# Mixer 1 attention with low keys on 128 rows, values as the stationary operand in two column groups, and one flat run of 48 steps per layer

## The chip, the cores and the metric

The kernel runs on one core of one Trainium2 chip, as one program. The metric is the device time of that core in microseconds (us), taken as the median of several executions. The names of the engines are those of the profile: PE is TensorE, PEld its weight loads, DVE is VectorE, ACT is ScalarE, POOL is GpSimd, SP is the queue from which the weights are fetched.

## The reference, cut to what matters

A sequence of 512 tokens of width 1024 goes through two layers of a first block and one layer of a second block, all in float32. Each layer of the first block is feed-forward, mixer, feed-forward, each behind an RMS norm:

```
x = x + 0.5 * swiglu(rmsnorm(x), gate, up, down)
proj = rmsnorm(x) @ w_in       # 256 pool columns, then q, k, v of 12 heads of 64
q, k = rope(q), rope(k)        # first 16 of the 64 channels
y = [pool(v_pool), attention(q, k, v)]
x = x + y @ w_out
x = x + 0.5 * swiglu(rmsnorm(x), gate2, up2, down2)
```

The attention of a head is a mixture of three dilated windows. The kernel computes it as one softmax over all 512 keys: exp(scale * (q.k + band)), where band holds the logarithm of how many of the three windows see a key, divided by the sum of those exponentials, times v. The second block (a gated part and a sparse attention) has its own code and isn't touched but for its norms.

## The kernel before, in words

Activations stand transposed, with channels on the 128 partitions and the 512 tokens along the free side, in 8 tiles (`x`, `xh`, `xl`). Every weight matrix is cut into units of 128 output columns by 1024 input rows. A unit is fetched by SP, split by POOL into a high part `wh` (L445) and a low part `wl` (L448) in two slots that alternate, and multiplied on PE in 8 blocks of three matmuls (L462 to L464: high times high, high weights times low activations, low weights times high activations). POOL may overwrite a slot once the unit before in that slot is used (`unit_used`). A layer has 66 units of the first feed-forward, 20 of the mixer's input projection (units 0, 1, 2 are q, k, v of head pair 0, units 3 and 4 the pool channels, then q, k, v of pairs 1 to 5), 8 of the output projection and 66 of the second feed-forward. Order on every engine is the order of the program; engines meet through semaphores only.

**Norm.** Before each projection ACT squares the 8 tiles of `x` into `sq` (SBUF, 4 buffers, L901), DVE adds them up in `rstd` (L1188, L1192), PE sums over partitions with a matmul with ones (`sum_of_sums`, L475, placed after the first four blocks of unit 2), and DVE and ACT make the inverse root in `rstd` (L1180, L905, L1182). In the mixer DVE also sets `padded` and `win` to zero ahead of the norm (L1415, L1416).

**Start of the mixer.** DVE makes `cosr` and `sinr`, turns q and k of pair 0 (`rope`: one product with `cosr`, L1263, four of 32 rows with `sinr`, L1266, one sum, L1271), evacuates v (L1294) and the two pool tiles (L1303), and forms the low parts `low_q` (L1280) and `low_k` (L1288) from the high parts that ACT has made (L927, L934). PE first does units 0 to 4. `proj_read` tells PE which banks were read.

**A pair of heads** is `pair_steps`, 8 steps: steps 0 to 3 are the four query tiles of head 0, steps 4 to 7 those of head 1. In a step PE computes the scores of 128 queries against 512 keys by two matmuls (`scores`): L588 with `qs` against `ks`, all 128 rows, which hold high and low queries above high keys twice, and L590 with the 64 rows of high queries against the 64 rows of `kl`. DVE adds the band and takes the row maximum (L1348), and negates it (L1351). ACT exponentiates with a row sum (L955). PE transposes the result in four tiles (`turn`, L597), ACT copies it to `pt` (L948), and PE multiplies with `pt` as weights and the 64 columns of `vtok` moving (`values`, L609), which gives 64 columns of bank 7 with tokens on partitions. Between these PE does the three units of the next pair in 24 blocks (`fill`), in counts of 3, 3, 3, 2, 2, 2, 1, 1 and, behind step 7, 2, 2, 1, 2. Turns trail scores by two steps and values by three. At the end of a pair the pipeline runs empty: the last turns and values, DVE's reciprocal and scaling (L1375, L1378), and PE's `turn_back` to channels (L562), which ACT and DVE split into `mh1` and `ml1` (L978 or L982, L1389). Pairs 0 to 3 are two passes of a hardware loop with two pairs in it; pair 5 has no fill. Then comes the output projection (`out_blocks`).

## Time and profile before

| | us |
|---|---|
| median of 3 runs (2848.26 to 2851.93) | 2850.3 |
| span of the profiled execution | 2847.3 |
| PE busy | 2701.1 (95%) |
| DVE busy | 1351.3 (47%) |
| ACT busy | 548.1 (19%) |
| POOL busy | 1477.8 (52%) |

Only the span is given for the profiled execution; what lies around it is taken as the difference to the median, 3.0 us. The page's chain that ended last puts 84% of the span on PE, 9% on DVE, 2% on ACT and 1% on POOL. The first layer's mixer lies between about 385 and 705 us of the span, the second layer's between about 1428 and 1746 us. In a row of the timeline the first two numbers are the start and the time in us, and brackets at the end give the engine's idle time just before and what ended it. PE's rows overlap, because its matmuls are pipelined: the cost of one is the distance between its start and the next one's. A call on float32 data (not the split kind) appears as two matmuls.

### The profile page before, as it was taken

The page shows a single profiled execution, that of the slowest core. Times are in us where ns is not written, and L with a number is a line of the kernel's source. Part 1 is how long each engine was busy: PE and PEld are TensorE (multiplying, and loading weights), DVE is VectorE, ACT ScalarE, POOL GpSimd, SP SyncE. Part 2 cuts the span into 40 slices and gives each one's busy share as a digit, 9 for nine tenths or more (in the row PEclk, how much of TensorE's full clock was granted, in tenths as well). Part 3 has the DMA queues.
Part 4 walks back from the last instruction along what each step waited for, and adds up shares of the span by engine and source line. Part 5 has one row for each costly group of instructions (what it writes and reads, how often), then busy time and mean ns, then how long its engine had stood idle before and what let it go on. Part 6 is the DMA issues. An engine that isn't in the chain of part 4 may idle for free.

```text
span 2847.3 us, 35053 instructions
## 1 busy us (share of the span) xinstructions
PE 2701.1 (95%) x12380; PEld 2179.0 (77%) x12380; DVE 1351.3 (47%) x1812; ACT 548.1 (19%) x996; POOL 1477.8 (52%) x828
## 2 busy tenths in 40 slices
PE   6999989989999999999989999999989889999998
PEld 5888867767888878888867768888866667788886
DVE  5555055564555215553075655555044566555512
ACT  2110014432111002110033432110021255211100
POOL 4666652225666656666642226666643400566663
PEclk9999999999999999999999999999999989999999
DMA  3222220111222222222210102222232200222221
GB/s 140 97 95 103 88 89 30 44 45 60 95 97 100 92 104 74 103 89 103 93 70 30 44 30 91 101 95 97 103 117 84 73 3 0 74 98 94 103 88 74
DMA packets 34366, 228.48 MB, mean 80 GB/s; under 512 B 5364, under 2 KB 6132, under 8 KB 7412
## 3 DMA queue, kind: packets, MB, share of 16 engines
q1 hardware_dynamic: 33140, 226.23, 22.0%
q10 hardware_dynamic: 1152, 1.29, 0.1%
q8 instruction: 43, 0.70, 0.1%
q14 instruction: 31, 0.25, 0.0%
HBM read 225.41 MB, written 2.10 MB: 80 GB/s over the span
## 4 chain that ended last, share of the span: by engine, by line
PE 84%; DVE 9%; issue 4%; ACT 2%; POOL 1%; DMA 0%; DVEq 0%; SPq 0%; ACTq 0%; POOLq 0%
PE bank L462 24%; PE bank L463 24%; PE bank L464 24%; PE bank L609 2%; DVE ropet L1266 1%; PE bank L590 1%; POOL wl L448 1%; DVE rstd L1192 1%; PE bank L839 1%; DVE qs L1280 1%; PE bank L597 1%; PE bank L588 1%; ACT ks L934 1%; DVE rstd L1182 1%; PE bank L712 1%
## 5 line engine op out<-in xcount | busy, mean ns | idle before, releaser
L445 POOL TENSOR_SCALAR wh<-raw 128x1024 fp32r<-128x1024 f32 x412 | 443.2, 1076 | 1307.4 <-PE bank L464 1227.8
L448 POOL TENSOR_TENSOR wl<-raw,wh 128x1024 fp32r<-128x1024 f32 x412 | 1034.8, 2512 | 34.4
L462 PE MATMUL bank<-xh,wh 128*128 128x512 f32 x2096 | 844.1, 403 | 15.9 <-DVEq L1306 10.9
L463 PE MATMUL bank<-xl,wh 128*128 128x512 f32 x2096 | 825.3, 394 | 0.0
L464 PE MATMUL bank<-xh,wl 128*128 128x512 f32 x2096 | 824.8, 394 | 0.0
L462 PEld LDWEIGHTS bank<-xh,wh 128*128 128x128 f32 x2096 | 398.5, 190 | 118.4 <-issue 32.0
L464 PEld LDWEIGHTS bank<-xh,wl 128*128 128x128 f32 x2096 | 398.5, 190 | 84.4
L463 PEld LDWEIGHTS bank<-xl,wh 128*128 128x128 f32 x2096 | 399.1, 190 | 79.9 <-issue 2.6
L464 PE MATMUL bank<-acth,wl 128*128 (+1 forms) x880 | 342.9, 390 | 0.0
L463 PE MATMUL bank<-actl,wh 128*128 (+1 forms) x880 | 342.9, 390 | 0.0
L462 PE MATMUL bank<-acth,wh 128*128 (+1 forms) x880 | 342.9, 390 | 0.0
L1203 DVE SCALAR_TENSOR_TENSOR x<-bank,x 128x512 f32<-128x512 f32 x64 | 43.9, 691 | 607.6 <-PE bank L464 607.6
L1231 DVE TENSOR_TENSOR un<-gn,un 128x512 f32<-128x512 f32 x110 | 310.1, 2819 | 0.0
L1221 DVE TENSOR_TENSOR un<-bank,rstd 128x512 f32<-128x512 f32 x110 | 76.0, 691 | 472.0 <-PE bank L464 472.0
L920 ACT ACTIVATE gn<-gn 128x512 f32<-128x512 f32 x110 | 69.6, 632 | 961.3 <-DVE gn L1221 961.3
L464 PEld LDWEIGHTS bank<-acth,wl 128*128 128x128 f32 x880 | 165.3, 188 | 34.3
L462 PEld LDWEIGHTS bank<-acth,wh 128*128 128x128 f32 x880 | 165.3, 188 | 34.2
L463 PEld LDWEIGHTS bank<-actl,wh 128*128 128x128 f32 x880 | 165.3, 188 | 34.0
L609 PE MATMUL bank<-vtok,pt 128*128 128x64 f32 x768 | 101.0, 277 | 29.7 <-ACT pt L948 28.5
L1230 DVE TENSOR_TENSOR acth<-gn,un 128x512 f32 (+1 forms) x110 | 123.8, 1126 | 0.0
L609 PEld LDWEIGHTS bank<-vtok,pt 128*128 128x128 f32 x768 | 96.6, 198 | 34.6 <-ACT pt L948 32.8
L1348 DVE CUSTOM_DVE_ANT_0 sc<-bank,band 128x512 f32<-128x512 f32 x96 | 66.4, 691 | 107.3 <-PE bank L590 104.2
(211 smaller groups left out, 2483.0 us busy)
## 6 DMA issues: line engine op xcount, KB each, us to landing
raw<-in_stream SPq DMA_DIRECT2D x206, 1024.0 KB, 4.8
x<-in_x SPq DMA_DIRECT2D x2, 1024.0 KB, 9.5
w<-in_w1k SPq DMA_DIRECT2D x1, 2048.0 KB, 8.1
w<-in_w1v SPq DMA_DIRECT2D x1, 2048.0 KB, 7.7
out_dram<-x SPq DMA_DIRECT2D x4, 512.0 KB, 2.7
invcount<-in_c_invcount ACTq DMA_DIRECT2D x1, 512.0 KB, 14.7
wst<-in_ws SPq DMA_DIRECT2D x1, 512.0 KB
band<-in_c_band ACTq DMA_DIRECT2D x1, 448.0 KB, 13.6
```

The lines of the kernel that those rows point to most:

```text
L445: nc.gpsimd.tensor_scalar(wh[:, h, :, :], src, 1.0, 1.0, ALU.mult, ALU.mult)\
L448: nc.gpsimd.tensor_tensor(wl[:, h, :, :], src, wh[:, h, :, :].bitcast(F32), ALU.subtract).then_inc(split_done, 1)
L462: mm = nc.tensor.matmul(bank, wh[:, slot, k, :], rh, start=start, stop=False)
L463: mm = nc.tensor.matmul(bank, wh[:, slot, k, :], rl, start=False, stop=False)
L464: return nc.tensor.matmul(bank, wl[:, slot, k, :], rh, start=False, stop=stop)
L609: mm = nc.tensor.matmul(B[7][:, c:c + HD], pt[:, s % 2, kt * P:(kt + 1) * P], vtok[:, e, kt, HD * a:HD * (a + 1)], start=(kt == 0), stop=( ...
L920: nc.scalar.activation(gn[:, e, :], gn[:, e, :], ACT.Silu).then_inc(silu_done, 1)
L1203: V.scalar_tensor_tensor(x[:, m, :], B[m][:, :], factor, x[:, m, :], ALU.mult, ALU.add)\
L1221: V.tensor_tensor(dst[:, e, :], B[2 * e + j][:, :], rstd[:, :], ALU.mult)\
L1230: V.tensor_tensor(h, gn[:, e, :], un[:, e, :], ALU.mult).then_inc(act_part, 1)
L1231: V.tensor_tensor(un[:, e, :], gn[:, e, :], un[:, e, :], ALU.mult).then_inc(act_part, 1)
L1348: V.tensor_tensor_reduce(sc[:, s % 4, :], B[(5, 2)[s % 2]][:, :], band[:, off:off + T], 1.0, -3.0e38, ALU.add, ALU.max, smax[:, s:s + 1]). ...
```

## The change

- **Scores.** `kl` becomes `[P, 2, 2, T]`: for each head its low keys lie in that head's 64 rows and the other 64 rows are zero. The second matmul takes all 128 rows of `qs`. POOL sets `kl`, `padded` and `win` to zero in each layer, between its split of units 67 and 68; DVE's two memsets go.
- **Values.** The 64 columns of `vtok` of a head are now the weights, and two turned tiles (256 queries) of `pt` or `sq` move. A half of a pair (4 steps) is 8 calls, heads alternating, into partitions 0 to 63 and 64 to 127 of bank 7. Steps go query tile by query tile, heads alternating in them.
- **Normalising.** Since the output has channels on partitions at once, the reciprocals are spread (`recb`, ACT), transposed by PE (`reciprocal_rows`), and multiplied by DVE with a copy of bank 7 that ACT has made (`on`, `numerators`, `normalise`). Low outputs are formed from two SBUF tiles (`low_output`).
- **Order.** The 48 steps of a layer run through without a break and without loops. Values, reciprocals and outputs of a pair are done within the steps of the next one. Fill is 4, 4, 4, 4, 2, 2, 2, 2. The evacuation of v and of the pool tiles moves from ahead of the first scores to behind the first maxima. The ten pool operations are spread over pairs 1 to 4. `sc` has 3 buffers for 4.
- **Norm.** All norms but two (6 and 9) put the squares into three free PSUM banks; DVE copies the first and adds seven.

```diff
-        kl = sb("kl", [P, 2, T], F32R, at=mix1)
+        kl = sb("kl", [P, 2, 2, T], F32R, at=mix1)
@@ POOL
-            with pool.Fori(0, U_ALL // 4) as i:
+            def split_units(i):
...
+            with pool.Fori(0, DEPTH) as l:
+                with pool.Fori(0, U_FFN // 4 + 1) as i:
+                    split_units(l * (U_LAYER // 4) + i)
+                nc.gpsimd.memset(kl[:, :, :, :].bitcast(F32), 0.0).then_inc(zeroed, 1)
+                nc.gpsimd.memset(padded[:, :, :], 0.0).then_inc(zeroed, 1)
+                nc.gpsimd.memset(win[:, :, :], 0.0).then_inc(zeroed, 1)
+                with pool.Fori(U_FFN // 4 + 1, U_LAYER // 4) as i:
+                    split_units(l * (U_LAYER // 4) + i)
@@ PE
-                        nc.tensor.matmul(B[(5, 2)[s % 2]][:, :], qs[h:h + HD, e, a, i:i + P], kl[h:h + HD, e, :],
-                                         start=False, stop=True).then_inc(s_done, 1)
+                    nc.tensor.matmul(o[:, :], qs[:, e, a, i:i + P], kl[:, e, a, :], start=False, stop=True)\
+                        .then_inc(s_done, 1)
+                def values(h):
+                    j, half = h // 2, h % 2
+                    if half == 0:
+                        pe.wait_ge(vtok_done, l * PAIRS + (j + 1))
+                        pe.wait_ge(num_done, l * PAIRS + (j + 1))
+                    pe.wait_ge(pte_done, l * STEPS + (4 * h + 6))
+                    q = 2 * P * half
+                    for kt in range(NQ):
+                        for a in range(2):
+                            r = slice(HD * a, HD * (a + 1))
+                            mm = nc.tensor.matmul(B[7][r, q:q + 2 * P], vtok[:, j % 2, kt, r], turned(h)[:, 4 * a + kt, :],
+                                                  start=(kt == 0), stop=(kt == NQ - 1))
+                    mm.then_inc(pv_done, 1)
+                for j in range(PAIRS):
+                    work = [(n, k) for n in range(3) for k in range(KT)] if j < PAIRS - 1 else []
                     for s in range(8):
+                        g = 8 * j + s
+                        if s == 0 and work:
+                            fill(j, work, FILL[s])
+                        scores(g)
+                        if s > 0 and work:
+                            fill(j, work, FILL[s])
                         if s == 1:
+                            value_turn(j)
+                        if g >= 2:
+                            turn(g - 2)
+                        if s == 2 and j > 0:
+                            values(2 * j - 1)
+                        if s == 3 and j > 0:
+                            reciprocal_rows(j - 1)
+                        if s == 6:
+                            values(2 * j)
+                        if j == PAIRS - 1 and s in (4, 5):
+                            pooled_map(s - 4)
+                turn(STEPS - 2)
+                turn(STEPS - 1)
...
                 pe.wait_ge(ml_done, l * 8 + 8)
-                out_blocks(0, range(KT - 1))
-                turn_back(l * PAIRS + 5)
-                out_blocks(1, range(4))
+                out_blocks(0, range(4))
+                values(HALVES - 1)
+                out_blocks(0, range(4, KT - 1))
+                reciprocal_rows(PAIRS - 1)
+                out_blocks(1, range(KT - 1))
@@ DVE, norm: to is the tuple of free banks
-                V.tensor_tensor(rstd[:, :], sq[:, 0, :], sq[:, 1, :], ALU.add).then_inc(sq_used, 2)
-                for m in range(2, KT):
+                V.tensor_copy(rstd[:, :], B[to[0]][:, :]).then_inc(sq_used, 1)
+                for m in range(1, KT):
-                    V.tensor_tensor(rstd[:, :], rstd[:, :], sq[:, m % 4, :], ALU.add).then_inc(sq_used, 1)
+                    V.tensor_tensor(rstd[:, :], rstd[:, :], B[to[m % 3]][:, :], ALU.add).then_inc(sq_used, 1)
@@ DVE, behind the maximum of step s of pair j
+                        if s == 0:
+                            v_out(l * PAIRS + j, ...)
+                        if j == 0 and s < 2:
+                            pool_out(s)
+                        if s == 1 and j > 0:
+                            reciprocals(j - 1)
+                        if s == 4 and j > 0:
+                            normalise(j - 1)
+                        if s in (2, 3) and more:
+                            rope(pair, 0, u, B[slot], s - 2)
+                        if s in (4, 5) and more:
+                            rope(pair, 1, u + 1, B[1 - slot], s - 4)
+                        if s == 5 and more:
+                            low_q(pair, 1 - e)
+                        if s == 6 and j > 0:
+                            low_output(j - 1, j)
                         if s == 7 and more:
+                            low_k(pair, 1 - e)
+                        if s in (0, 1, 6) and 1 <= j <= 4:
+                            n = (j - 1) * 3 + (0, 1, 6).index(s)
+                            if n < len(pool_ops):
+                                pool_op(n)
@@ ACT, behind the exponential of step s of pair j
+                        if s == 1 and j > 0:
+                            spread_reciprocals(j - 1)
+                        if s == 3 and j > 0:
+                            numerators(j - 1)
+                        if s == 4 and more:
+                            high_q(l * PAIRS + (j + 1), 1 - e)
+                        if s == 5 and j > 0:
+                            high_output(j - 1)
+                        if s == 6 and more:
+                            high_k(l * PAIRS + (j + 1), 1 - e)
```

## Rows read from the trace of the kernel before

**Rows 1.** Windows: stretch and length, busy of PE, PEld, DVE, ACT, POOL, PEclk, DMA share, GB/s.
```profile
433.50:651.70 218.20, 203.35 (x1076) 156.36 (x1074) 128.69 (x257) 90.26 (x188) 53.52 (x30) 0.94 0.11 39
429.40:434.00 4.60, 4.51 (x10) 3.15 (x10) 2.74 (x4) 1.12 (x1) 0.00 (x0) 0.50 0.00 0
```
**Rows 2.** Timeline of PE, step 3 of pair 1, and the next scores.
```profile
484.47 0.48 PE L588 MATMUL bank<-ks,qs 128*128 128x512 f32 x1
484.88 0.50 PE L590 MATMUL bank<-kl,qs 64*128 64x512 f32 x1
485.31 0.50 PE L462 MATMUL bank<-xh,wh 128*128 128x512 f32 x1
485.65 0.40 PE L463 MATMUL bank<-xl,wh 128*128 128x512 f32 x1
485.89 0.39 PE L464 MATMUL bank<-xh,wl 128*128 128x512 f32 x1
...
486.81 0.60 PE L597 MATMUL bank<-ident,sc 128*128 128x128 f32 x4
487.24 1.00 PE L609 MATMUL bank<-vtok,pt 128*128 128x64 f32 x8
488.06 0.48 PE L588 MATMUL bank<-ks,qs 128*128 128x512 f32 x1
```
**Rows 3.** Timeline of PE, pair ends with their idle time, and two starts in pair 5.
```profile
506.59 1.97 PE L609 MATMUL bank<-vtok,pt 128*128 128x64 f32 x8 [2.79 <-ACT pt L948]
...
545.35 1.11 PE L609 MATMUL bank<-vtok,pt 128*128 128x64 f32 x8 [0.65 <-ACT pt L948]
...
641.83 0.48 PE L588 MATMUL bank<-ks,qs 128*128 128x512 f32 x1
643.96 0.48 PE L588 MATMUL bank<-ks,qs 128*128 128x512 f32 x1
```
**Rows 4.** The chain of waits, in order of time: start, us, what.
```profile
2187.09 7.05 PE bank L712 x32
```
**Rows 5.** Timeline of PE: two diagonal tiles, and two column groups in blocks of eight.
```profile
634.23 1.08 PE L634 MATMUL bank<-padded,poolw_now 64*64 64x512 f32 x4
2226.33 2.57 PE L761 MATMUL bank<-wst,gvtok 128*64 128x128 f32 x32
```
**Rows 6.** Groups by line, 433.5 to 632.5: count, busy us, mean ns, idle before.
```profile
L955 ACT ACTIVATE sc<-sc,sneg 128x512 f32<-128x512 f32 x40 | 28.7, 718 | 26.1 <-DVE sneg L1351 26.0
L1348 DVE CUSTOM_DVE_ANT_0 sc<-bank,band 128x512 f32<-128x512 f32 x41 | 28.3, 691 | 46.3 <-PE bank L590 44.9 <-DVE qs L1280 0.9
```
**Rows 7.** Timeline of DVE at the end of pair 1.
```profile
493.68 4.31 DVE L1280 TENSOR_TENSOR qs<-qk,qs 64x512 fp32r<-64x512 f32 x2
...
506.09 1.40 DVE L1288 TENSOR_TENSOR kl<-qk,ks 64x512 fp32r<-64x512 f32 x2 [2.65 <-ACT ks L934]
```
**Rows 8.** Line L1192 by itself: ns min/median/max, first and last start.
```profile
L1192 DVE TENSOR_TENSOR rstd<-rstd,sq x48: 691/693/2759, 28.0 to 2475.5; 128x512 f32<-128x512 f32 x48
```
**Rows 9.** Timeline at the start of mixer 1, first layer: DVE, then PE.
```profile
394.12 0.94 DVE L1415 MEMSET padded<- 128x1056 f32 x1 [0.17 <-issue]
...
405.96 1.25 PE L475 MATMUL bank<-rstd,ones 128*128 128x512 f32 x2 [3.94 <-DVE rstd L1192]
429.49 0.79 PE L462 MATMUL bank<-xh,wh 128*128 128x512 f32 x1 [7.17 <-DVEq L1306]
```
**Rows 10.** Timeline of ACT ahead of the first scores.
```profile
426.63 2.58 ACT L934 ACTIVATE ks<-qk 64x512 fp32r<-64x512 f32 x4 [4.16 <-DVE qk L1271]
```
**Rows 11.** POOL: the split of unit 68 (timeline), and the page's group of low parts.
```profile
394.77 1.05 POOL L445 TENSOR_SCALAR wh<-raw 128x1024 fp32r<-128x1024 f32 x1 [5.34 <-PE bank L487]
...
L448 POOL TENSOR_TENSOR wl<-raw,wh 128x1024 fp32r<-128x1024 f32 x412 | 1034.8, 2512 | 34.4
```
**Rows 12.** Timeline of PE at the start of block 2.
```profile
2133.14 1.24 PE L475 MATMUL bank<-rstd,ones 128*128 128x512 f32 x2 [2.65 <-DVE rstd L1192]
2149.54 9.53 PE L712 MATMUL bank<-w,blk 128*62 128x256 f32 x32 [5.51 <-DVE blk L1532]
```

More of the change, by code:

```diff
@@ L556, in mixer1, with fill @@
                     unit_blocks(u0 + n, n % 2, bank, range(KT))
-                def turn_back(pair):
-                    pe.wait_ge(otok_done, pair + 2)
+                def fill(j, work, count):
+                    slot = (1 + j) % 2
+                    for n, k in [work.pop(0) for _ in range(count)]:
+                        if k == 0:
+                            pe.wait_ge(proj_read, l * U_PROJ + (2 if j == 0 and n < 2 else j * 3 + (4 + n)))
+                        unit_blocks(u0 + (5 + j * 3 + n), (slot + n) % 2, B[(slot + n) % 2], [k])
@@ L965, in pair_steps @@
+                        if s == 4 and more:
[4 more added lines that the diff above has]
+                            high_k(l * PAIRS + (j + 1), 1 - e)
+                        if s >= 6 and not more:
+                            t = s - 6
                             act.wait_ge(poolmm_done, l * 2 + (t + 1))
@@ L1341, in pair_steps, with low_output @@
+                def low_output(j, done):
+                    dve.wait_ge(mh_done, l * 8 + done)
+                    V.tensor_tensor(ml1[:, 2 + j, :], on[:, :], mh1[:, 2 + j, :].bitcast(F32), ALU.subtract)\
+                        .then_inc(ml_done, 1)
+                for j in range(PAIRS):
+                    e, more = j % 2, j < PAIRS - 1
+                    pair, u = l * PAIRS + (j + 1), u0 + (5 + j * 3)
+                    slot = (1 + j) % 2
                     for s in range(8):
-                        i = s % 4
@@ L1355, in pair_steps @@
-                        if s == 6 and more:
-                            low_q(pair + 1, 1 - e)
-                        if s == 7 and more:
-                            rope(pair + 1, 1, u + 1, B[1 - slot], 0)
-                        for n in range(len(pool_ops) * s // 8, len(pool_ops) * (s + 1) // 8) if pooled else ():
-                            after, o, in0, in1, op = pool_ops[n]
-                            dve.wait_ge(pool_step, ps + after)
-                            V.tensor_tensor(o, in0, in1, op).then_inc(pool_step, 1)
@@ L1363, in pair_steps @@
-                        if s in (4, 6) and not more:
-                            t = s // 2 - 2
-                            dve.wait_ge(mh_done, l * 8 + (t + 6))
-                            V.scalar_tensor_tensor(ml1[:, t, :], B[t][:, :], poolscale_now[:, t:t + 1],
-                                                   mh1[:, t, :].bitcast(F32), ALU.mult, ALU.subtract)\
-                                .then_inc(ml_done, 1)
-                    if more:
-                        rope(pair + 1, 1, u + 1, B[1 - slot], 1)
-                        low_k(pair + 1, 1 - e)
@@ L1381, in pair_steps @@
-                    if more:
-                        v_out(pair + 1, u + 2, B[slot])
-                def output(done, at):
-                    h, lo = mh1[:, at, :], ml1[:, at, :]
-                    if not isinstance(at, int):
-                        h, lo = h.rearrange("p a t -> p (a t)"), lo.rearrange("p a t -> p (a t)")
-                    dve.wait_ge(mh_done, done)
-                    V.tensor_tensor(lo, B[6][:, :], h.bitcast(F32), ALU.subtract).then_inc(ml_done, 1)
-                with dve.Fori(0, 2) as it:
-                    for e in range(2):
-                        pair_steps(it * 2 + e, e, True)
-                        output(l * 8 + it * 2 + (e + 1), bass.ds(it * 2 + (2 + e), 1))
@@ new lines, in mixer1 @@
+                        if s == 7 and more:
+                            low_k(pair, 1 - e)
[3 more added lines that the diff above has]
+                                pool_op(n)
+                        if s == 7 and not more:
+                            pool_low(0)
+                pool_low(1)
+                reciprocals(PAIRS - 1)
+                normalise(PAIRS - 1)
```

337 lines of the change are left out of this document (152 added, 185 removed).

## The prediction

> **What bounds the kernel now.** The page comes first: PE is busy 95% of the span and holds 84% of the chain that ended last, so time goes only where PE's own work shrinks or where PE stands idle. The windows come second. In the first layer's attention, 433.5 to 651.7, PE is busy 203.4 of 218.2 us, at a mean granted clock of 0.94 of full speed [rows 1]. So 14.8 us are idle, and some of the rest runs at the lower of the two levels, 1.2 GHz instead of 2.4: the stretch behind the first wait stands at 0.50 over 4.6 us [rows 1], so each such stretch loses about 2.3 us. Third is the timeline of one step, read by the distances of starts [rows 2]. In plain blocks a matmul costs 0.23 to 0.24 us (485.65 to 485.89; 0.23 below). The first scores matmul costs 0.41, the second, on 64 rows, 0.43, and the block's first one behind it 0.34. The four transposes cost 0.43 (486.81 to 487.24), the values of one step 0.82 (487.24 to 488.06). Fourth are the waits at the ends of pairs: 2.79 and 0.65 us idle [rows 3]. Behind 2.79 the eight value matmuls show 1.97 us and behind 0.65 only 1.11, so the long wait also cost the clock and the short one did not.
>
> As a check, the ledger of these 48 steps before: scores and the block behind 48 x 1.18, of which 0.23 belongs to the block, 45.6; 117 blocks x 0.69, 80.7; turns 48 x 0.43, 20.6; values 48 x 0.82, 39.4; turns of v and of outputs 11 x 0.36 (an estimate, a little under the 0.43 of the same four transposes), 4.0; two pool maps 2.5, from 1.08 each [rows 5] and a start. That makes 192.8. With 14.8 idle and four to five clock losses of 2.3 it gives 217 to 219, against 218.2.
>
> **Scores.** Both matmuls now fill 128 rows, as do the blocks around them. I price them as blocks: 0.46 a step instead of 0.95, so 48 x 0.46 = 22.1 instead of 45.6, 23.5 less a layer. The bounds are 0.46 and 0.95 (if what costs is something other than the 64 rows); I take the first, because everything else in the sequence that is 128 by 128 and split runs at 0.23 [rows 2].
> The Trainium skill, TensorEngine Tiling (Array Packing), Key Properties, says that a change of the tiling mode drains TensorE. By that rule the extra 0.49 us is two drains a step and goes, as I have it; but the rule also puts two drains around each half of the values.
>
> **Values.** A half is 8 calls, 16 matmuls of 256 moving columns. The same width on 62 weight columns takes 7.05 us for 32 [rows 4], 0.220 each, with weight loads hidden: 3.53 a half one after the other, 1.76 if the two column groups run fully side by side. Two rows bear on that [rows 5]. The pool map has two 64x64 tiles on the diagonal, four matmuls of 512 columns, which at the same rate would be 1.76 in series; it shows 1.08. Two column groups of 128x64 in blocks of eight show 2.57 for 32 matmuls of 128 columns, where the rate makes 3.53. So they do overlap, and the more they alternate the more so; here they alternate with every call. I take 1.76 and 0.39 for entry and exit (0.18 and 0.11 above the plain 0.23 in rows 2, and 0.1 for the lone first matmul), 2.15 a half. Eleven of the twelve halves lie in the 48 steps (23.7), the last between the output blocks. Twelve make 25.8 for 39.4: 13.6 less a layer. Ends: 1.76 and 3.92.
> The Trainium skill, TensorE: Matmul & The Clock Gate, The mechanism, states that a weight load overlaps running matmuls only where the row group differs, and here both heads use all rows; by that each matmul would pay its load too. The row of 62 weight columns contradicts it, since 0.220 a matmul leaves no room for a load between them, and I give it no chance.
>
> **The rest of PE's work.** Pair 0's first four blocks now come ahead of scores 0, so 116 blocks remain, 80.0. Turns stay 20.6, small turns 4.0, pool maps 2.5. Sum of the 48 steps: 22.1 + 80.0 + 20.6 + 23.7 + 4.0 + 2.5 = 152.9.
>
> **What waits then.** ACT needs about 1.5 a step, 0.72 for the exponential [rows 6] and by estimate 0.2 for reading its sum and 0.6 for a copy of the same width; that is 12 of 28 us a pair and 6 more for its other copies: no bound. DVE needs about 0.95 a step for maximum and negation [rows 6], and 0.69 for every operation that reads a bank: 7.6 + 12 x 0.7 for both ropes + 1.4 + 1.4 for the low parts + 0.7 each for v, normalising and low output + 2.5 to 3.5 of pool operations, 24 us a pair. With two SBUF operands it takes 0.69 alone and 2.76 beside POOL's low part [rows 8]; `low_q` took 4.31 for two [rows 7]. So 24 to 28 us against PE's 28.6: near, and it matters how it lies. The late half is tight. Put scores 4 of a pair at 0. PE's steps 4, 5 and 7 have two blocks (0.46 + 1.38 + 0.43 = 2.27), step 6 has 4.42 with values, and four blocks (2.76) stand ahead of the next scores: these could start at 14.0. DVE does maximum 4 to 1.6, normalises to 2.3, three rope reads to 4.4, maximum 5 to 5.4, two rope reads and the sum to 7.6, `low_q` to 9.1, maximum 6 to 10.0. ACT exponentiates to 11.0 and makes the high keys, 2.58 [rows 10], to 13.6. `low_k` takes 1.4 [rows 7]: 15.1. That is 1.1 us late. POOL splits the next unit from about 11 to 14.5, so `low_k` or the pool operation ahead may run slow; I take 2.0 us a boundary, between 0 and 4.9. An idle of 2.0 is nearer 0.65 without clock loss than to 2.79 with it [rows 3], less clearly than I would like. Five boundaries: 10. In the last pair, without fill, a step took 2.13 (641.83 to 643.96 [rows 3]); shorter scores leave ACT's 1.5 and the round trip, 1.65 by estimate. Its eight steps and pool parts come to 17 for 14.5 of work, 2.5 idle, and 1.2 more until the second pool tile's low part lets the output blocks start. Sum: 152.9 + 10 + 3.7 = 166.6, and 2.15 for the last half behind: 168.8 against 218.2, 49.4 less. The second layer repeats the first within 1 us. Two layers: 98.8.
>
> **Ahead of the attention.** PE waits 3.94 us for DVE's sum of squares [rows 9]. Its adds take up to 2.76 beside POOL [rows 8], behind two memsets that begin at 394.1 [rows 9]. A read of a bank takes 0.69 [rows 6], some 0.78 with its semaphore. Eight from 394.1 end at 400.3, before PE gets there at 402.0 (405.96 - 3.94). The wait goes, no more: 3.9, and about 0.4 because the sum's own matmuls (1.25 for two) no longer run at the lower clock, an estimate. Then v and the pool tiles leave the path: high keys end at 426.63 + 2.58 = 429.2 [rows 10], `low_k` at 430.7, and scores started at 433.5, so 2.8 less. PE still idles before its first fill (7.17 us before [rows 9]): v's evacuation no longer counts there but q's and k's banks do, so it idles about 4.5, and four slow blocks end just before `low_k` does. Start: 7.1 a layer, 14.2 in all.
> POOL's three memsets, 4160 elements a partition, stand in its idle 5.34 us [rows 11]. At POOL's fastest row, 1.05 us for 1024, they take 4.3 and fit; at its slower one, 2.51 for 1024 [rows 11], 10.2, which holds unit 68 back by 4.9 and eats the 3.9. A plain write is nearer the first, so 0.
> Block 2's norm saves PE's 2.65, and DVE's chain to the next wait of 5.51 moves with it [rows 12]: 2.7. The feed-forward norms gain nothing: PE has blocks to do there and shows no wait at its sum. Longer straight code on all engines: nothing, since no long wait of the trace names instruction fetch.
>
> **Sum.** 98.8 + 14.2 + 2.7 = 115.7. The profiled execution spans 2847.3; with the 3.0 between span and median, 2850.3 - 115.7 = 2734.6, say 2735.
>
> **Rivals.**
> 1. *The column groups don't overlap.* A half costs 3.92. For it: two groups in blocks of eight saved only 27% of the series. Against it: the diagonal tiles. 24 x 1.77 = 42 more: 2777.
> 2. *DVE is late at every boundary and the clock goes with it.* Idle 4.9 instead of 2.0, and 2.3 of lower level, ten times: 52 more, 2787. For it: DVE's 24 to 28 of 28.6 us, `low_q` at 4.31. Against: POOL has its split done before `low_q`.
> 3. *The scores gain nothing*, what costs is not the 64 rows: 47 more, 2782. Against it: the jump from 0.23 to 0.41 is seen nowhere between tiles of one shape in rows 2.
> 4. *Slower.* Short waits in every step hold the granted clock at the lower level through the attention. PE's 152.9 become 305.8; with the same waits and last half that is 324 a layer against 218.2, 106 more, twice 212, less 17 for starts and norm: 3045. It needs 0.50 as in rows 1 over the whole stretch; it decides from about 37% of the work (168.8 + 0.37 x 152.9 exceeds 218.2 + 7.1). Against it: the last pair waits a little in every step and its scores still show 0.48, the full speed's value [rows 3].
>
> **How the numbers follow.** Forecast 0.66 with its own range of 2708 to 2765 (boundaries 0 to 20 less, or 15 more; memsets up to 9 more; last pair 6 either way); rival 1 0.11, rival 2 0.13, rival 3 0.07, rival 4 0.03. The range of 2700 to 2785 takes in 1 and 3 and part of 2. A measurement tells 0.2%, about 6 us, from no change; only rival 4 lies beyond, and only a mild form of it near zero: faster 0.96, same 0.01, slower 0.03.
>
> **What would show it.** The attention stretch of about 169 us with the last half, at a clock near 0.97. Scores' two starts 0.23 apart; 16 value matmuls within 2.2 us (3.9 would be rival 1). L475 in both mixers without a wait and eight DVE reads of 0.69 before it. POOL idle between memsets and unit 68. PE idle at scores of step 0 behind `kl`, 1 to 3 us; over 4 with half-speed blocks behind it would be rival 2. A time above 2785 or below 2700 would mean that a term of this sum is wrong by a third.

## The result, and the profile after

The changed kernel takes 2745.5 us (median of 4 runs, 2743.2 to 2751.3) against 2849.6 for the kernel before on the same chip, a ratio of 0.9639 [0.9627, 0.9651]. The forecast was 2735, with an own range of 2708 to 2765. The forecast started from 2850.3, the median of three runs before; the profiled execution of the changed kernel took 2747.0, 103.3 less than that. The spans of the two profiled executions differ by 102.1, where 115.7 was forecast.

First the page of the changed kernel: the span, the busy times, and the chain that ended last by engine.

```profile
span 2745.2 us, 34077 instructions
...
PE 2612.7 (95%) x11996; PEld 2109.0 (77%) x11996; DVE 1314.9 (48%) x1816; ACT 559.2 (20%) x1018; POOL 1480.5 (54%) x834
...
PE 84%; DVE 7%; issue 4%; ACT 2%; POOL 2%; DMA 0%; DVEq 0%; SPq 0%; ACTq 0%; POOLq 0%
```

PE still bounds the kernel: it is busy 95% of the span and holds 84% of the chain, both as before. Where the 102.1 came from is read by setting the same events of both traces side by side, PE's starts in us (the last column is the difference of the two lengths):

| stretch | before | after | change | forecast |
|---|---|---|---|---|
| up to mixer 1, layer 1 | 389.48 | 388.64 | -0.8 | 0 |
| start of mixer to first scores, layer 1 | 44.0 | 34.8 | -9.2 | -7.1 |
| the same, layer 2 | 41.8 | 34.8 | -7.0 | -7.1 |
| first scores to output blocks, layer 1 | 218.3 | 174.3 | -44.0 | -51.6 |
| the same, layer 2 | 218.6 | 174.3 | -44.3 | -51.6 |
| output blocks to feed-forward 2, layer 1 | 49.8 | 53.8 | +4.0 | +2.15 |
| the same, layer 2 | 49.8 | 56.5 | +6.7 | +2.15 |
| the four later feed-forward stretches together | | | -1.3 | 0 |
| block 2 to its first L734 (L712 before) | 36.2 | 32.3 | -4.0 | -2.7 |
| rest of block 2 | | | -2.2 | 0 |

So the direction of every large term is right. The attention gained 7.3 to 7.6 us a layer less than forecast, and the stretch behind it cost more than forecast.

Windows of the changed kernel: stretch and length, busy of PE, PEld, DVE, ACT, POOL, PEclk, DMA share, GB/s. The first answers to [rows 1].

```profile
423.40:597.70 174.30, 159.30 (x865) 122.07 (x865) 122.67 (x260) 93.70 (x198) 54.52 (x30) 0.97 0.14 49
...
482.00:486.00 4.00, 3.71 (x13) 3.00 (x14) 2.68 (x7) 1.41 (x3) 0.00 (x0) 0.68 0.00 0
574.00:582.00 8.00, 4.87 (x17) 3.85 (x18) 4.41 (x10) 3.50 (x8) 1.69 (x1) 0.60 0.36 131
```

PE is busy 159.3 of 174.3 us, at 0.97 of the full clock against 0.94. The idle time is still 15.0, as before (14.8): the waits moved and did not go. Two short stretches stand at the lower level in part, 482 to 486 and 574 to 582. Before there were four in this layer's attention (from 468, 506, 584 and 622) and the end of one that began ahead of it.

The timeline of PE in the changed kernel: start, us, instruction, idle time just before. It answers to [rows 2].

```profile
459.87 1.95 PE L631 MATMUL bank<-sq,vtok 128*64 128x256 f32 x16
461.75 0.50 PE L600 MATMUL bank<-ks,qs 128*128 128x512 f32 x1
...
560.98 0.48 PE L600 MATMUL bank<-ks,qs 128*128 128x512 f32 x1
561.29 0.39 PE L601 MATMUL bank<-kl,qs 128*128 128x512 f32 x1
561.52 0.40 PE L489 MATMUL bank<-xh,wh 128*128 128x512 f32 x1
...
562.91 0.60 PE L616 MATMUL bank<-ident,sc 128*128 128x128 f32 x4
563.26 0.48 PE L600 MATMUL bank<-ks,qs 128*128 128x512 f32 x1
```

A step with two blocks takes 563.26 - 560.98 = 2.28 us; the forecast had 2.27. Inside it the first scores matmul costs 0.31, the second 0.23 and the block's first one 0.23, together 0.77; before the three cost 0.41, 0.43 and 0.34, together 1.18. Whether the 64 rows are the cause of that is tested below. A half of the values costs 461.75 - 459.87 = 1.88, and 2.09 with the longer turn ahead of it (0.53 for 0.35) and the 0.02 that the scores behind it are dearer; the forecast had 2.15.

The same timeline, now the rows with idle time. It answers to [rows 3].

```profile
451.03 0.49 PE L600 MATMUL bank<-ks,qs 128*128 128x512 f32 x1 [1.92 <-DVE kl L1326]
...
482.29 0.49 PE L600 MATMUL bank<-ks,qs 128*128 128x512 f32 x1 [2.21 <-DVE kl L1326]
...
484.00 0.63 PE L489 MATMUL bank<-xh,wh 128*128 128x512 f32 x1
...
546.20 0.49 PE L600 MATMUL bank<-ks,qs 128*128 128x512 f32 x1 [2.16 <-DVE kl L1326]
...
577.08 0.79 PE L600 MATMUL bank<-ks,qs 128*128 128x512 f32 x1 [4.63 <-DVE kl L1326]
...
596.24 0.66 PE L616 MATMUL bank<-ident,sc 128*128 128x128 f32 x4 [1.14 <-ACT sc L994]
597.67 0.49 PE L489 MATMUL bank<-mh,wh 128*128 128x512 f32 x1 [0.78 <-DVE ml L1380]
...
614.45 0.50 PE L489 MATMUL bank<-mh,wh 128*128 128x512 f32 x1 [3.05 <-POOL wl L463]
```

At four boundaries PE waits 1.9 to 2.2 us for the low keys (at 515.01, not shown, 2.10); the forecast had 2.0. At the fifth it waits 4.63 and then works at half speed. Behind the wait of 2.21 it does too (the row of a block's matmul shows 0.63 at 484.00, and 0.39 to 0.40 at full speed), behind those of 1.92, 2.10 and 2.16 it does not. In the second layer the four waits are 1.95, 2.17, 2.05 and 2.19, and there it is the one of 2.05, at 1506.29, that has half-speed blocks behind it. Last, it waits 3.05 for POOL in the output blocks, where 1.11 stood before.

What is late there is read from the timelines of DVE, ACT and POOL at the fifth boundary.

```profile
562.22 0.69 DVE L1408 CUSTOM_DVE_ANT_0 sc<-bank,band 128x512 f32<-128x512 f32 x1 [1.21 <-PE bank L601]
...
569.10 1.40 DVE L1318 TENSOR_TENSOR qs<-qk,qs 64x512 fp32r<-64x512 f32 x2
570.72 0.69 DVE L1408 CUSTOM_DVE_ANT_0 sc<-bank,band 128x512 f32<-128x512 f32 x1 [0.22 <-PE bank L601]
...
574.96 1.99 DVE L1326 TENSOR_TENSOR kl<-qk,ks 64x512 fp32r<-64x512 f32 x2 [1.92 <-ACT ks L959]
...
571.64 0.72 ACT L994 ACTIVATE sc<-sc,sneg 128x512 f32<-128x512 f32 x1 [2.91 <-DVE sneg L1411]
...
572.36 2.57 ACT L959 ACTIVATE ks<-qk 64x512 fp32r<-64x512 f32 x4
...
573.35 2.35 POOL L463 TENSOR_TENSOR wl<-raw,wh 128x1024 fp32r<-128x1024 f32 x1
```

The chain is the one of the forecast: maximum 4, the ropes, `low_q`, maximum 6, exponential 6, high keys, low keys. `high_k` needs only `qk`, which was ready at 569.0, but it stands behind exponential 6 in ACT's order, and ACT is idle 2.91 us ahead of that. `low_k` ends at 576.95, 14.7 us behind maximum 4's start and 16.0 behind the scores of step 4 (560.98); its first part runs beside POOL's `wl` (1.99 for 1.40).

### The profile page after: what moved, and what is told of

It is laid out like the page before. It is cut to its first block, busy times and chain, and to the rows that moved or that the text cites. A ratio compares the mean times of both kernels' runs of the same rounds, so it can differ in the third digit from the quotient of the medians.

```text
span 2745.2 us, 34077 instructions
## 1 busy us (share of the span) xinstructions
PE 2612.7 (95%) x11996; PEld 2109.0 (77%) x11996; DVE 1314.9 (48%) x1816; ACT 559.2 (20%) x1018; POOL 1480.5 (54%) x834
## 4 chain that ended last, share of the span: by engine, by line
PE 84%; DVE 7%; issue 4%; ACT 2%; POOL 2%; DMA 0%; DVEq 0%; SPq 0%; ACTq 0%; POOLq 0%
PE bank L489 25%; PE bank L491 25%; PE bank L490 25%; POOL wl L463 1%; PE bank L631 1%; DVE ropet L1304 1%; PE bank L861 1%; PE bank L616 1%; PE bank L600 1%; ACT ks L959 1%; PE bank L601 1%; DVE rstd L1219 1%; PE bank L508 1%; PE bank L734 1%; POOL wh L460 1%
## 5 line engine op out<-in xcount | busy, mean ns | idle before, releaser
L489 PE MATMUL bank<-xh,wh 128*128 128x512 f32 x2096 | 825.7, 394 | 6.8 <-DVEq L1308 5.5
L935 ACT ACTIVATE xh<-x,gain 128x512 fp32r<-128x512 f32 x48 | 32.5, 719 | 314.7 <-DVE x L1240 314.7
L1270 DVE TENSOR_TENSOR actl<-un,acth 128x512 f32 (+1 forms) x110 | 86.5, 786 | 13.3
## 6 DMA issues: line engine op xcount, KB each, us to landing
invcount<-in_c_invcount ACTq DMA_DIRECT2D x1, 512.0 KB, 14.7
```

The costliest lines, as they stand in the source:

```text
L489: mm = nc.tensor.matmul(bank, wh[:, slot, k, :], rh, start=start, stop=False)
L1270: V.tensor_tensor(lo, un[:, e, :], h.bitcast(F32), ALU.subtract).then_inc(act_done, 1)
```

## The experiments

Each ran beside the kernel before on the same chip (2849.2 to 2849.3 in all three batches, 7 runs each); every kernel had 4 runs. The changed kernel ran again only beside the last batch (2746.7 there, 2745.5 here), so in the first two a difference from it is one between chips. "Full-clock sum" is span times mean granted clock: what the span would be had PE never been at the lower level. It is 2776.1 before and 2693.0 after, so of the 102.1 about 83 are work and waits and 19 are clock (by the third digit of the clock, within 3). No run puts the new values or the flat order of the steps alone into the kernel before: their shares of the 102.1 are read from the traces.

### The 64 rows put back

```diff
-  nc.tensor.matmul(o[:, :], qs[:, e, a, i:i + P], kl[:, e, a, :], start=False, stop=True)
+  r = slice(HD * a, HD * (a + 1))
+  nc.tensor.matmul(o[:, :], qs[r, e, a, i:i + P], kl[r, e, a, :], start=False, stop=True)
```

> The changed kernel with its second scores matmul back on the 64 rows of one head; all else stays. The ledger prices 0.49 us a step, 96 steps, 47 us. My theory: the waits of 2.1 us ahead of step 0's scores in the changed kernel are waits for DVE and ACT, not for PE, so four longer steps of the late half of a pair use them up. Then the time rises by 47 less about 20, to some 2770 to 2777, and the waits for kl all but vanish. Rival: waits and PE's work simply add, and the time rises by the whole 47, to 2792. If what costs is not the 64 rows, it stays at 2745.

Measured: 2797.2 (2791.9 to 2800.1), ratio 0.9810 [0.9793, 0.9826]: 52 above the changed kernel, more than the theory (2770 to 2777) and than its rival (2792). Timeline of PE in this kernel (L602 is the second scores matmul):

```profile
545.88 0.48 PE L600 MATMUL bank<-ks,qs 128*128 128x512 f32 x1
546.29 0.49 PE L602 MATMUL bank<-kl,qs 64*128 64x512 f32 x1
546.71 0.50 PE L489 MATMUL bank<-xh,wh 128*128 128x512 f32 x1
...
548.57 0.48 PE L600 MATMUL bank<-ks,qs 128*128 128x512 f32 x1
```

The step is 2.69 for 2.28: 0.41, and 96 of them make 39. The waits for the low keys gave back only 2.6 of that (28.3 to 25.7 in twelve: ten boundaries and the first scores of each layer). At four boundaries of a layer they are 1.5 to 1.6 instead of 1.9 to 2.2, and no less, since POOL's split, which PE's last block releases, now lay exactly beside `low_k`; DVE and POOL in this kernel:

```profile
559.72 3.47 DVE L1327 TENSOR_TENSOR kl<-qk,ks 64x512 fp32r<-64x512 f32 x2 [1.09 <-ACT ks L960]
...
559.86 2.78 POOL L463 TENSOR_TENSOR wl<-raw,wh 128x1024 fp32r<-128x1024 f32 x1
```

The rest is clock: 0.974 over the span. The full-clock sum rose by only 32.5 of the 53.1 by which the spans differ, so some 20 us more than in the changed kernel are lost to the lower level. Part of it comes behind the shorter waits. PE in this kernel:

```profile
491.13 0.49 PE L600 MATMUL bank<-ks,qs 128*128 128x512 f32 x1 [1.60 <-DVE kl L1327]
...
494.80 0.63 PE L490 MATMUL bank<-xl,wh 128*128 128x512 f32 x1
```

Behind a wait of 1.59 at 527.98 it is the same, behind waits of 1.51 and 1.60 at 457.33 and 563.32 the blocks run at full speed.

### The padding alone, in the kernel before

```diff
-  kl = sb("kl", [P, 2, T], F32R, at=mix1)
+  kl = sb("kl", [P, 2, 2, T], F32R, at=mix1)
+  nc.gpsimd.memset(kl[:, :, :, :].bitcast(F32), 0.0).then_inc(zeroed, 1)    # behind unit 67
-  ... qs[h:h + HD, e, a, i:i + P], kl[h:h + HD, e, :],
+  ... qs[:, e, a, i:i + P], kl[:, e, a, :],
```

> The kernel before with kl padded to 128 rows alone (zeroed by POOL in its idle time of each layer). Ledger: 47 us of PE's work less. Theory: the waits at pair ends (2.79, 0.65, 2.79, 5.19 us) hang on DVE and ACT work that starts with the scores of steps 6 and 7, so only what lies ahead of them gains: 28 to 38 us less, 2812 to 2822, with waits at pair ends that are longer by about 1 us each. Rival: all 47 come through, 2803.

Measured: 2827.4 (2825.6 to 2829.7), ratio 0.9927 [0.9910, 0.9943], 22 less, where the theory wanted 28 to 38. A step with two blocks and values fell from 3.59 to 3.19 (L598 from 480.66 to 483.85). That is 0.40, 39 for 96. The waits at the pairs' ends took 9 of it back, by the rows of who waited for `pt`, here and before:

```profile
PE bank L619: 37.6, 10
```
```profile
PE bank L609: 28.5, 10
```

The full-clock sum fell by 27.4, and the clock went from 0.975 to 0.973: longer waits (3.2 us at each of four ends instead of 0.65 to 2.81), and behind each a stretch at half speed. The padding is worth 22 in the old order of work and 52 in the new one. Most of that difference is clock: by the full-clock sums it is worth 27.4 and 32.5 (each within 3).

### Values: the order of the calls, and a single column group

```diff
-                    for kt in range(NQ):
-                        for a in range(2):
+                    for a in range(2):
+                        for kt in range(NQ):
```
and, on top of it, with the first head's output of each pair left out because the second one overwrites it:
```diff
-  nc.tensor.matmul(B[7][r, q:q + 2 * P], vtok[:, j % 2, kt, r], ...
+  nc.tensor.matmul(B[7][0:HD, q:q + 2 * P], vtok[:, j % 2, kt, r], ...
```

> The changed kernel with the eight calls of a half ordered head by head, four of one column group and then four of the other. Theory (overlap depends on alternation, as in blocks of eight of two column groups before, 73% of the series): 16 matmuls of a half take about 2.6 us instead of 1.88; of 24 x 0.7 = 17 us the waits for kl take up about 7, so 2752 to 2758. Rival (the queue ahead of the array is deep enough for four calls): no change, 2745.

> The changed kernel with both heads' values written to partitions 0 to 63, so that no second column group is used; the attention output of the first head of each pair is left out by that. Theory: 16 matmuls take 3.53 us instead of 1.88, 1.65 more a half, 40 in all, of which the ten late halves give back about 16 from the waits for kl: 2767 to 2772. Rival (the column groups never overlapped and 1.88 comes from elsewhere): no change.

Measured: head by head 2769.1 (2765.3 to 2779.7), ratio 0.9713 [0.9697, 0.9729], 24 above the changed kernel; one group 2780.8 (2779.7 to 2781.1), ratio 0.9757 [0.9741, 0.9773], 35 above. Timelines of PE, first head by head, then one group:

```profile
498.40 2.86 PE L631 MATMUL bank<-sq,vtok 128*64 128x256 f32 x16
501.19 0.50 PE L600 MATMUL bank<-ks,qs 128*128 128x512 f32 x1
```
```profile
494.80 3.67 PE L631 MATMUL bank<-sq,vtok 128*64 128x256 f32 x16
498.39 0.50 PE L600 MATMUL bank<-ks,qs 128*128 128x512 f32 x1
```

The same sixteen matmuls cost 1.88 when the column groups alternate, 2.79 in two blocks of eight, 3.59 in one group. So 0.91 and 1.71 a half, 22 and 41 over 24 halves. The first agrees with the 24 measured. Both expectations (2752 to 2758, 2767 to 2772) were too small, for they counted on the waits to absorb more; head by head they absorbed nothing (28.3 to 29.1 for the low keys), with one group some (28.3 to 22.9).

### Where the squares lie

```diff
-                dst = B[to[m % 3]][:, :] if to else sq[:, m % 4, :]
+                dst = sq[:, m % 3, :] if to else sq[:, m % 4, :]
...
-                    V.tensor_tensor(rstd[:, :], rstd[:, :], B[to[m % 3]][:, :], ALU.add).then_inc(sq_used, 1)
+                    V.tensor_tensor(rstd[:, :], rstd[:, :], sq[:, m % 3, :], ALU.add).then_inc(sq_used, 1)
```

The converse, squares into three banks and one copy with seven adds, was put alone into the kernel before.

> The changed kernel with the squares of all norms back in SBUF, three buffers. Theory: DVE's adds contend with POOL again (0.69 to 2.7 us each), PE waits again at the sum of squares of both mixers and of block 2, and the time rises by 12 to 17 us, to 2757 to 2762. Rival: the mixers' start gained because v and pool evacuations left the path and not by the norm; then the rise is under 5.

> The kernel before with the squares of its norms in PSUM banks alone (its two memsets on DVE stay). The undone norm in the changed kernel cost 20 us, more than the 12 to 17 that its waits explain. Theory: the memsets (0.94 us each) still stand ahead of the adds, so PE waits some 0.3 us instead of 3.9 at the mixers' sums and 0 at block 2's; with the shifts behind and the lower clock that goes, 12 to 16 us less: 2833 to 2837. Rival: it is worth 20 here too, 2829.

Measured: squares back in SBUF 2765.6 (2760.2 to 2766.6), ratio 0.9699 [0.9682, 0.9715], 20 above the changed kernel, where 12 to 17 were expected. Banks alone in the kernel before 2832.0 (2831.6 to 2834.5), ratio 0.9943 [0.9926, 0.9960], 17 less, one past the expected 12 to 16. The line of the adds by itself, in the changed kernel and with the squares in SBUF (ns min/median/max); it answers to [rows 8]:

```profile
L1229 DVE TENSOR_TENSOR rstd<-rstd,bank x56: 686/687/690, 28.0 to 2373.8; 128x512 f32<-128x512 f32 x56
```
```profile
L1229 DVE TENSOR_TENSOR rstd<-rstd,sq x56: 691/693/2754, 27.7 to 2393.0; 128x512 f32<-128x512 f32 x56
```

No add with a bank as one operand took over 690 ns; with two SBUF operands they took up to 2754, and the seven adds ahead of the first mixer 10.61 us instead of 5.23. The Trainium skill, SBUF — State Buffer, Who interferes with whom, says that a VectorE instruction with at most one SBUF input, outside its 2-port modes, does not contend with GpSimd, and that one with two contends with a GpSimd instruction that reads SBUF, not with one that only writes it. The two rows agree with the first two statements. So does a stretch of `squares_in_sbuf` with the third: from 389.85 five of DVE's `xl`, with two SBUF inputs, run beside POOL's memsets in 3.39 us, 0.68 each.

With the squares in SBUF PE waits again, 9.8 us in three places (3.21 at 404.34), and from the start of the mixer to the first scores it takes 40.3 instead of 34.8: 5.6 a layer, of which the wait itself is 3.2; the sum's two matmuls, which then fall to the lower level, are 1.1 more in the first layer. Block 2's stretch up to L734 is 4.5 longer, which makes 15.7 in three places; the rest of the 20 was not followed. In the kernel before, banks alone bring that stretch of a mixer to 38.2 in both layers, from 44.0 and 41.8.

### The wait for the low keys taken away

`high_k` goes ahead of exponential 6 on ACT, `low_k` to step 6 and `low_output` to step 7 on DVE.

```diff
+                        if s == 6 and more:
+                            high_k(l * PAIRS + (j + 1), 1 - e)
                         act.wait_ge(neg_done, l * STEPS + (g + 1))
...
-                        if s == 6 and j > 0:
-                            low_output(j - 1, j)
-                        if s == 7 and more:
+                        if s == 6 and more:
                             low_k(pair, 1 - e)
+                        if s == 7 and j > 0:
+                            low_output(j - 1, j)
```

> The changed kernel with two moves: ACT makes the high keys ahead of the exponential of step 6 instead of behind it, and DVE makes low_k behind the maximum of step 6 and the low output behind that of step 7. Theory: ACT idles 2.5 us before that exponential while the keys are ready, and this order makes PE wait 2.1 us at four boundaries and 4.6 at the fifth. The four waits go and the fifth halves, and no boundary costs the clock: 20 to 28 us less, 2717 to 2725. Rival: the wait moves to the next in line (exponential or maximum behind it) and under 8 us come through.

Measured: 2724.2 (2722.7 to 2726.0), ratio 0.9561 [0.9545, 0.9577], 21 less than the changed kernel, as expected. The boundary waits are gone but for 0.36 at the fifth; first scores to output blocks take 163.1 for 174.3. One new wait appears in each layer. DVE, POOL and PE in this kernel:

```profile
565.27 2.85 DVE L1394 TENSOR_TENSOR ml<-on,mh 128x512 fp32r<-128x512 f32 x1
...
565.21 2.36 POOL L463 TENSOR_TENSOR wl<-raw,wh 128x1024 fp32r<-128x1024 f32 x1
...
569.60 0.66 PE L609 MATMUL bank<-ident,vraw 128*128 128x128 f32 x4 [3.63 <-DVE vraw L1332]
```

`low_output` now meets POOL's `wl` (2.85 for 0.69), and v's evacuation, two places behind it, is late. So the chain named above was the cause of the boundary waits, fifth one included. The waits for the low keys fall from 28.3 to 4.7, the two new waits take back 7.3, and the rest of the 21 is clock (0.983 for 0.981).

### Work in front of the fifth boundary

The blocks of pair 4's steps are 4, 4, 4, 4, 1, 1, 1, 5 instead of 4, 4, 4, 4, 2, 2, 2, 2, to lay more of them behind the last scores.

```diff
+FILL_LAST = (4, 4, 4, 4, 1, 1, 1, 5)
...
-                            fill(j, work, FILL[s])
+                            fill(j, work, (FILL if j < PAIRS - 2 else FILL_LAST)[s])
```

> The changed kernel with the fill of pair 4 alone set to 4, 4, 4, 4, 1, 1, 1, 5, so that three blocks more stand ahead of pair 5's first scores, which have no fill of their own. Theory: the wait there is 4.6 us for want of cover; three blocks of 0.69 take it to about 2.6, and the half-speed stretch behind it goes: 3 to 4.5 us a layer, 2736 to 2739. Rival: PE reaches later maxima earlier and waits as much in steps 5 to 7: no change.

Measured: 2747.8 (2743.3 to 2752.6), ratio 0.9645 [0.9628, 0.9662], no difference (2 apart, inside the spread of both), as its rival said. The wait is 4.63 as before, at 577.95: the chain runs from the scores of step 4 and takes 16 us from there, and PE had the same blocks for it in either order.

### POOL's slot in the output blocks

```diff
-                out_blocks(1, range(KT - 1))
+                out_blocks(1, range(4))
                 pe.wait_ge(ml_done, l * 8 + 9)
                 out_blocks(0, [KT - 1])
-                out_blocks(1, [KT - 1])
+                out_blocks(1, range(4, KT))
```

> The changed kernel with the output projection's unit 1 cut as before: four blocks, then the last block of unit 0, then the other four. Theory: POOL can then split unit 2 two us sooner and PE waits 1.1 instead of 3.05 us for it, and in the second layer the lower clock behind that wait goes: 2 and 4.5 us, 2738 to 2740. Rival: the last low output is not ready after four blocks, and the wait only moves to there: no change.

Measured: 2740.1 (2739.7 to 2741.1), ratio 0.9619 [0.9603, 0.9635], 5.4 less. The wait falls from 3.05 to 1.05 in each layer (at 614.06 and 1604.59), and the half-speed blocks behind it in layer 2 are gone. In the profiled execution layer 2's output stretch is 4.7 shorter and layer 1's only 0.4, since there half-speed blocks stand in it now (from 598.6). So the term exists, and its cause is that the last block of output unit 0 comes behind seven blocks of unit 1: it frees POOL's slot for unit 2 only then.

### Together

In the next batch the changed kernel ran again, beside two combinations. The first has `high_k` and `low_k` early, `low_output` left in step 6 behind `low_k`, and the sooner slot; the second adds the fill of `cover_last_pair`.

> The changed kernel itself once more, on the chip of its neighbours here, so that they can be set against it: 2743 to 2749.

> High keys ahead of the exponential of step 6, low_k and then the low output both behind the maximum of step 6, and the output projection's unit 1 cut in two. The early-keys run left one wait of 3.6 us in each layer, for v's evacuation in pair 5, behind a low output that took 2.85 us beside POOL's split and a maximum that came late for it. Theory: one step earlier the low output runs before the split begins, at 0.69, that wait goes to about 1, and with 5.4 us from the slot the sum is 2724 - 5 - 5 = 2714 (2710 to 2719). Rival: the three gains overlap, and the time stays at 2719 or above.

> As the run beside it, and the fill of pair 4 set to 4, 4, 4, 4, 1, 1, 1, 5. In the changed kernel that gave nothing, since the wait ran from the scores of step 4 and the blocks were moved within that stretch. Theory: the same here, within 2 us of its neighbour. Rival: with the chain shortened PE's own order counts again, and 2 to 4 us come through.

Measured: changed kernel 2746.7 (2742.9 to 2751.7), ratio 0.9642 [0.9626, 0.9658]; first combination 2723.2 (2722.7 to 2724.0), ratio 0.9559 [0.9544, 0.9575]; second 2721.6 (2720.9 to 2722.6), ratio 0.9555 [0.9539, 0.9570]. Both beat the kernel before and the changed one, the first by 23.5 where 21 and 5 would add to 27. So its theory (2710 to 2719) fell and its rival's time (2719 or above) held; part of what is missing is a wait that neither change had alone. The second is within 2 us of the first, as expected. The waits of PE in the first combination, 424 to 597: us in total, times, longest.

```profile
PE bank L600 <- DVE smax L1408: 5.5, 4, 1.6
PE bank L600 <- DVE kl L1326: 1.6, 2, 1.3
...
```

With `low_k` and `low_output` both in step 6, the maximum of step 7 is late: PE waits 1.57, 1.48 and 1.59 us at the three boundaries where a pool operation stands in DVE's step 6 too (2.76 beside POOL's `wl`, at 477.78), 0.82 at the last, where none does, and not at all at the first, where `low_output` isn't there either. The window of the second combination over the attention has a clock of 1.00:

```profile
420.00:600.00 180.00, 170.23 (x935) 130.77 (x934) 129.86 (x266) 98.97 (x205) 58.58 (x32) 1.00 0.13 48
```

So the waits of up to 1.6 us cost their own length in this run and nothing more. That is no rule: in `scores_64_rows` waits of 1.59 and 1.60 had half-speed blocks behind them.

## Why the prediction was right, point by point

- **Scores**, 23.5 a layer forecast. Mechanism right, size 0.40 to 0.41 a step and not 0.49: 19.5. "I price them as blocks: 0.46 a step" misses that the first scores matmul costs 0.31, not 0.23. It stands behind the transposes of float32 data; a block's matmul in that place costs the same 0.31 (446.10 to 446.41).
- **Values**, 2.15 a half: measured 1.88, 2.09 with entry and exit. The groups overlap by 1.7 us of 3.59, and the guess that alternating matters is shown by 2.79. Rival 1 (3.92 a half) falls by the 2.09; the matmuls cost 3.59 only when one group is used. The Trainium skill, TensorE: Matmul & The Clock Gate, The mechanism, says that a weight load overlaps matmuls in flight only where the row group differs (though it names a background weight buffer too). The trace doesn't agree: here all sixteen use the same rows, each load shows 0.136 us, and sixteen with their matmuls take 1.88; in one group it is 0.224 a matmul, where [rows 4] has 0.220.
- **48 steps of PE's work**, 152.9: the window has 159.3 busy. About 4 of that is the lower clock at 482 and 574 to 582; the scores are 4 dearer, and the turns cheaper, 0.35 to 0.36 for 0.43, which is 3 back. With the 0.7 of the values about 2 of the 6.4 stay without a term.
- **Boundaries**, 2.0 each, 10: four are 1.92, 2.21, 2.10 and 2.16. The chain has the links that were laid out; at the fifth boundary it takes 16.0 us from the scores of step 4 where 15.1 was forecast, and 0.6 of the 0.9 is `low_k` beside POOL's `wl`, the slow run for which the forecast had put the same 0.9 on top. The fifth is 4.63. This is a step that failed: "four blocks (2.76) stand ahead of the next scores" is not true of the last pair, which has no fill; 2.0 + 2.76 = 4.8 would have been the term. With the half speed behind it, it costs some 5 a layer more than forecast.
- **Clock.** "An idle of 2.0 is nearer 0.65 without clock loss" was half right: in each layer one of four such waits had half-speed blocks behind it, three had not. Rival 2 wanted 4.9 and a loss at each of five; it came at one boundary, the fifth.
- **Last pair**, 2.5 and 1.2 idle: 1.14 and 0.78. Together the attention took 174.3 for 166.6: 3.0 more wait, 4 clock, 2.4 work, less 1.8 here.
- **Output blocks**, +2.15: +4.0 and +6.7. The missed step is POOL's slot: "the last half behind" was priced on PE alone, and where block 7 of unit 0 lies had not been followed to POOL, 3.05 for 1.11. In layer 2 the clock took 2.7 more. `free_slot_sooner` shows it.
- **Start**, 7.1 a layer: 9.2 and 7.0. The after side is the same in both, 34.77; the before side was 44.0 and 41.8. The difference lies with DVE: in the first layer more of its operations with two SBUF operands ran beside POOL's `wl` (412.76 to 415.46), and PE waited 7.17 behind them, 3.77 in the second. DVE in the kernel before, first layer, then second:

```profile
413.14 2.88 DVE L1254 TENSOR_TENSOR sinr<-sin,rstd 128x512 f32<-128x512 f32 x1
...
1456.25 1.53 DVE L1254 TENSOR_TENSOR sinr<-sin,rstd 128x512 f32<-128x512 f32 x1
```

  With `before_squares_in_banks` this stretch is 38.2 in both layers, so the squares in banks are worth 5.8 and 3.6 of it, and the rest of the change there (v, the pool tiles and DVE's two memsets off the path) 3.4. The forecast had 4.3, the memsets with it, and 2.8. The rows that carry the steps, POOL, DVE and PE in the changed kernel (they answer to [rows 9] and [rows 11]):

```profile
388.52 1.82 POOL L470 MEMSET kl<- 128x2048 f32 x1
...
393.86 1.05 POOL L460 TENSOR_SCALAR wh<-raw 128x1024 fp32r<-128x1024 f32 x1 [1.68 <-PE bank L514]
...
393.81 5.23 DVE L1229 TENSOR_TENSOR rstd<-rstd,bank 128x512 f32<-128x512 f32 x7
...
400.31 1.02 PE L502 MATMUL bank<-rstd,ones 128*128 128x512 f32 x2
417.70 0.49 PE L489 MATMUL bank<-xh,wh 128*128 128x512 f32 x1 [2.72 <-DVEq L1308]
423.41 0.50 PE L600 MATMUL bank<-ks,qs 128*128 128x512 f32 x1 [1.11 <-DVE kl L1326]
```

  The memsets cost nothing, as POOL is still idle 1.68 behind them. The eight reads end at 399.0, forecast 400.3, and PE's sum has no wait. PE is idle 2.72 where 4.5 was forecast, and 1.11 ahead of the first scores where none was.
- **Block 2's norm**, 2.7: 4.0. Up to the sum it is 3.2 less, of which 2.65 are the wait; the sum's matmuls no longer follow a wait and run at 1.02 for 1.24, and the stretch from there to L734 is 0.8 shorter. The 2.2 in the rest of block 2 was not followed further; 1.1 of it are waits for `qs` (17.0 to 15.9).
- **Rival 3** (scores gain nothing) falls by `scores_64_rows` and `before_padded`. **Rival 4** (slower, lower clock throughout) falls by the 0.97.

The saving is 13.6 short of the forecast. Against it stand, a layer, 4.0 in the scores, 5 at the fifth boundary, 1.7 of clock at one other, about 3 in the output blocks and 2 of PE's work that no term accounts for; for it 3 in the turns, 1.8 in the last pair, 0.7 in the values and 1 at the start, and once 1.3 in block 2's norm and 4.3 in stretches that were forecast at 0. That the two sides offset each other is luck: with the first side alone the forecast of 2735 would have become about 2766, at the edge of its range (2765). Three steps of the prediction failed in their own terms: the first scores matmul at a block's price, the fifth boundary at the price of the others, and the output blocks without POOL's slot.

Open: why 2.21 us at 482 cost half speed and 2.10 at 515 and 2.16 at 546 did not. PE's rows ahead of the three are alike, blocks at 0.23 with no gap. The length does not decide it: in the second layer it was 2.05 and not 2.17 or 2.19, and in the first layer of `free_slot_sooner`, whose attention is the same code, 1.95 and one of 2.16, and not the other 2.16 or 2.05.

## What to carry to other kernels

Lay the late chain of a software pipeline out from the last event that starts it, and do so for each boundary by itself: the last round has no cover, and a wait there costs its length and then the clock. A matmul over part of the rows among full ones can cost more than it saves. What padding it with zeros is worth hangs on the order of work around it, here 22 or 52, the more so as waits and clock move with it: price it in the order in which it will run. When matmuls go to two column groups, alternate them call by call; and put one operand of a VectorE addition into a free bank where GpSimd reads SBUF beside it.

## What was not expected of the hardware

- Sixteen matmuls of 256 columns on 128x64 tiles take 1.88, 2.79 or 3.59 us by order and group alone. A load is 136 to 137 ns on average, and none of it shows: in one group a matmul takes 0.224.
- A lone 64-row matmul in a run of 128-row ones costs 0.40 to 0.41 us beyond its own width; this is told twice, in two orders of work. The Trainium skill, TensorEngine Tiling (Array Packing), Key Properties, has a change of mode drain TensorE without a price. By the measured step two changes are 0.41; the two around each half of the values, where only the columns change, are about 0.2 (2.09 - 1.88).
- GpSimd's memset of 2048 elements a partition takes 1.82 us, 0.89 ns an element, faster than any of its rows of before (1.05 for 1024).
- A saving on PE can lengthen a wait and lose clock: `before_padded` spared 39 us of steps and ended 22 faster; `scores_64_rows` added 39 and ended 52 slower.
